# Second feed-forward of a hybrid layer: gate pairs by seven block products, with an up tile ahead of the last two

## What is computed

```python
def swiglu(x, w_gate, w_up, w_down):
    return (jax.nn.silu(x @ w_gate) * (x @ w_up)) @ w_down

x = layer_norm(ALPHA * x + 0.5 * swiglu(x, ffn1_w_gate, ffn1_w_up, ffn1_w_down), ln1_g, ln1_b)
...
x = layer_norm(ALPHA * x + mixed @ w_o, ln2_g, ln2_b)
x = layer_norm(ALPHA * x + 0.5 * swiglu(x, ffn2_w_gate, ffn2_w_up, ffn2_w_down), ln3_g, ln3_b)
```

## Time and profile before

| | |
|---|---|
| median of 3 runs | 2640.41 us |
| the profiled execution | 2638.99 us |
| its span | 2637.2 us |
| TensorE busy, weight loads busy | 98%, 92% of the span |
| VectorE, ScalarE, GpSimd busy | 51%, 31%, 41% |
| mean granted TensorE clock | 0.995 |
| matmuls | 19924 |

### The profile page before, as it was taken

The page is one execution under the profiler, slowest core; times in us unless marked ns, Lnnn a source line. Parts: engine busy times, 40 slices in busy tenths (PEclk is TensorE's granted clock), DMA queues, the critical chain, the costliest instruction groups (busy, mean ns, idle before and its releaser), DMA issues.

```text
span 2637.2 us, 50055 instructions
## 1 busy us (share of the span) xinstructions
PE 2595.3 (98%) x19924; PEld 2432.5 (92%) x19924; DVE 1350.2 (51%) x2181; ACT 807.7 (31%) x1354; POOL 1077.8 (41%) x528
## 2 busy tenths in 40 slices
PE   9999999999999999999999999999999999999997
PEld 9999999998899999999999999999977788888887
DVE  7665554964443452323476655449644435523236
ACT  3222224235532242222252222242355322422222
POOL 4444435413234454434354444354132444544442
PEclk9999999999999999999999999999999999999999
DMA  5333324312233323333233323243122233333332
GB/s 161 95 90 89 88 80 105 81 29 59 60 84 84 104 83 94 88 94 90 80 107 90 96 86 91 80 105 81 27 61 67 76 95 92 96 96 96 96 95 64
DMA packets 457350, 226.58 MB, mean 86 GB/s; under 512 B 42385, under 2 KB 456337, under 8 KB 457201
## 3 DMA queue, kind: packets, MB, share of 16 engines
q1 hardware_dynamic: 450880, 217.09, 29.5%
q10 hardware_dynamic: 6320, 7.41, 1.0%
HBM read 220.20 MB, written 2.10 MB: 84 GB/s over the span
## 4 chain that ended last, share of the span: by engine, by line
PE 88%; DVE 6%; issue 3%; POOL 1%; DMA 1%; ACT 1%; SPq 0%; POOLq 0%; ACTq 0%; DVEq 0%
PE ps L569 74%; PE ps L680 4%; PE ps L592 3%; PE ps L836 1%; PE ps L922 1%; PE ps L961 1%; POOL w_lo L483 1%; DMA w_raw<-in_ffn_w_gate 1%; PE ps L937 1%; PE ps L926 1%; PE ps L843 1%; DVE stat L1727 1%; DVE s_state L1756 1%; DVE s_back L1766 0%; PE ps L939 0%
## 5 line engine op out<-in xcount | busy, mean ns | idle before, releaser
L483 POOL TENSOR_TENSOR w_lo<-w_raw,w_hi 128x1024 fp32r<-128x1024 f32 (+3 forms) x472 | 1038.1, 2205 | 1424.5 <-ACT w_hi L1080 1424.3
L1080 ACT ACTIVATE w_hi<-w_raw 128x1024 fp32r<-128x1024 f32 (+2 forms) x472 | 451.2, 960 | 839.5 <-PE ps L569 642.7
L569 PE MATMUL ps<-x_hi,w_hi 128*128 128x264 f32 (+2 forms) x3584 | 543.6, 302 | 2.0 <-DVE stat L1722 1.7
L569 PE MATMUL ps<-x_hi,w_lo 128*128 128x264 f32 (+2 forms) x3584 | 536.6, 300 | 0.9 <-POOL w_lo L483 0.9
L569 PE MATMUL ps<-x_lo,w_hi 128*128 128x264 f32 (+2 forms) x3584 | 536.3, 300 | 0.0
L569 PEld LDWEIGHTS ps<-x_hi,w_hi 128*128 128x128 f32 x3584 | 481.3, 188 | 29.4 <-issue 3.3
L569 PEld LDWEIGHTS ps<-x_hi,w_lo 128*128 128x128 f32 x3584 | 481.3, 188 | 24.1 <-POOL w_lo L483 1.7
L569 PEld LDWEIGHTS ps<-x_lo,w_hi 128*128 128x128 f32 x3584 | 481.3, 188 | 22.4
L1549 DVE TENSOR_TENSOR hid_rest<-hid_rest,ps 128x528 f32<-128x528 f32 (+1 forms) x88 | 61.6, 699 | 507.2 <-PE ps L569 486.9
L1551 DVE TENSOR_TENSOR hid_lo<-hid_rest,hid_hi 128x528 fp32r<-128x528 f32 (+1 forms) x88 | 224.3, 2548 | 3.1
L1080 ACT ACTIVATE hid_rest<-ps 128x528 f32 (+3 forms) x88 | 53.5, 608 | 354.5 <-PE ps L569 341.1
(11 more groups left out here) (306 smaller groups left out, 2969.5 us busy)
## 6 DMA issues: line engine op xcount, KB each, us to landing
w_raw<-in_ffn_w_gate SPq DMA_DIRECT2D x88, 512.0 KB, 3.8
w_raw<-in_ffn_w_up SPq DMA_DIRECT2D x88, 512.0 KB, 3.8
w_raw<-in_w_in SPq DMA_DIRECT2D x82, 512.0 KB, 3.9
w_raw<-in_ffn_w_down SPq DMA_DIRECT2D x64, 512.0 KB, 4.1
w_raw<-in_ffn_w_down SPq DMA_DIRECT2D x32, 384.0 KB, 3.3
w_raw<-in_w_o SPq DMA_DIRECT2D x16, 512.0 KB, 4.1
w_raw<-in_conv_w_out SPq DMA_DIRECT2D x16, 256.0 KB, 2.8
w_raw<-in_w_in SPq DMA_DIRECT2D x16, 256.0 KB, 2.9
```

The lines of the kernel that those rows point to most:

```text
L483: pool.tensor_tensor(w_lo[:, s, 0:n], w_raw[:, c % RAW, 0:n], w_hi[:, s, 0:n].bitcast(f32), ALU.subtract).then_inc(w_split, 1)
L569: ins = nc.tensor.matmul(dst, w[:, s, cols], x[:, k0 + k, tokens], start=first and k == 0 and n == 0, stop=last and k == n_tiles - 1 and n ...
L1080: return nc.scalar.activation(out, in_, f, **kw)
```

## The change

In the second feed-forward of both layers, two neighbouring gate tiles are made together by Winograd's form of Strassen's scheme: the weights (1024 rows by 256 columns) are cut into two halves of the rows by two tiles, the tokens into two halves, and the 2x2x2 block products become seven. This is done for 10 of the 11 pairs of a layer (`N_CROSS`); the first pair still goes through `first_products`. A block product is 4 weight tiles by 3 passes by 264 (or 256) tokens: 12 matmuls.

VectorE makes four sums of weight blocks for each pair (`add_weights`, L1842, from the raw pair `w_pair` into `w_sum`) and, once for each layer, four sums of input blocks and their low parts (`turn_inputs` and `turned_rest`, L1819 to L1830). It also puts the seven results together in PSUM (`combine`, L1862, five steps). ScalarE saves one result (`crossed_first`), rounds the seven half-size weight chunks and applies silu twice. GpSimd splits seven chunks of 128x512 beside the two up chunks. `w_hi` and `w_lo` become rings of eight half slots (`lay_ring`); ScalarE rounds a chunk when the chunks that held its place are done (`round_at`). For the last group of a part these are: down chunk 0 after block product 5, down chunk 1 after up tile 1, down chunk 2 after block product 7. Loads through `w_raw` keep their rule (two such chunks back must be split), but the gate pairs now have buffers of their own. The L1557 additions are gone; one 128x2112 addition (L1819) does their work ahead of the first product of the feed-forward's VectorE program.

The diff, cut to its core; its pieces are in turn SyncE's loads, TensorE, ScalarE, VectorE before (the removed additions) and VectorE now:

```diff
+FORM_AT, UP_AT = [0, 1, 2, 3, 4, 6, 7], [5, 8]
...
+            def ffn_crossed(l, b0, wg, wu, wd):
...
+                        group += 1
+                        if group < N_CROSS:
+                            load_pair(group)
+                        for j in range(2):
+                            load(l, c + UP_AT[j], 0, 8 * P, rows(wu, l, 0, KD, (f0 + 2 * q + j) * P, P), KD)
...
+            def crossed(l, part, q, a, t0):
...
+                if q == 0:
+                    pe.wait_ge(z_taken, t0 + 1)
+                else:
+                    pe.wait_ge(silu_done, a + 1)
+                pe.wait_ge(turned_ready, l * 4 + 1)
+                form(0, 1, turned(0), True)
+                form(1, 0, own(low, first), True)
...
+                form(2, 3, turned(1), True)
+                pe.wait_ge(turned_ready, l * 4 + 3)
+                form(3, 2, turned(2), True)
+                pe.wait_ge(first_kept, g + 1)
+                form(4, 0, own(high, first), False)
...
+                up(0)
+                pe.wait_ge(turned_ready, l * 4 + 4)
+                pe.wait_ge(crossed_step, 5 * g + 2)
+                form(5, 2, turned(3), False)
+                pe.wait_ge(crossed_step, 5 * g + 3)
+                form(6, 1, own(high, second), False)
+                up(1)
...
                     else:
                         pe.wait_ge(silu_done, n0 + (nf + 2))
+                        if w:
+                            pe.wait_ge(hid_done, n0 + (nf + 1))
                         layer_norm_first(l, 2 * w)
...
+            def ffn_crossed(l, b0):
...
+                        round_at(l, c)
+                        round_at(l, c + 1)
+                        act.wait_ge(chunk_done, done_at(l, c + 1))
+                        ACTV(kept[:, 0:sp.half], ps[:, 0, 0:sp.half]).then_inc(first_kept, 1)
+                        for k in range(2, UP_AT[1]):
+                            round_at(l, c + k)
+                        act.wait_ge(crossed_step, 5 * g + 5)
+                        silu(2 * q, apart(0, sp), 1.0)
+                        silu(2 * q + 1, apart(1, sp), -1.0)
+                        round_at(l, c + UP_AT[1])
...
-                        if w == 1 and part == 0:
-                            for k in ((f,), (f, f + 2))[f >= 4]:
-                                cols = sp.halves[0]
-                                tt(z[:, k, cols], xhf[:, k, cols], xlf[:, k, cols], ADD)
...
+                def turn_inputs():
+
+                    dve.wait_ge(x_ready[0], (n + 2) * KD)
+                    st.done(tt(z[:, :, first], xhf[:, :, first], xlf[:, :, first], ADD))
+                    dve.wait_ge(ln_out[1], (n + 1) * KD)
+                    b11, b12, b21, b22 = z[:, low, first], z[:, low, second], z[:, high, first], z[:, high, second]
+                    follow(tt(raw[:, 0], b11, b12, SUB), turned_made, l * 4 + 1)
...
+                        combine(l * N_CROSS + m, c)
+                        if m < N_CROSS - 1:
+                            add_weights(m + 1, range(4))
+                        hidden(part, f, c + UP_AT[0], 2)
+                        if part == len(PARTS) - 1 and f == nf - 2:
+                            layer_norm_shift(sp)
+                        hidden(part, f + 1, c + UP_AT[1], 3)
```

More of the change, by code:

```diff
@@ L533, in _ @@
                 norm(l, 1, B_FFN2)
-                ffn(l, B_FFN2)
+                for c in range(B_FFN2 + SLOTS, CH):
+                    split(l, c)
                 norm(l, 2, CH)
@@ L679, in last_tiles @@
                             for k in range(nk):
-                                ins = nc.tensor.matmul(ps[:, bank, 0:sp.half], w[:, s, k * P:(k + 1) * P],
+                                ins = nc.tensor.matmul(ps[:, bank, 0:sp.half], held(w, c + d, k * P, (k + 1) * P),
                                                        x[:, k, sp.halves[h]], start=p == 0 and k == 0,
@@ L687, in last_tiles, with form, up @@
                             spread_root(n, 0)
+            def crossed(l, part, q, a, t0):
+                c, g, sp = B_FFN2 + GROUPS_AT[part, q], l * N_CROSS + GROUP_OF.index((part, q)), stream(l)
+                first, second = sp.halves
+                low, high = slice(0, KD // 2), slice(KD // 2, KD)
+                turned = lambda n: [v[:, n, :, 0:sp.half] for v in (turned_hi, turned_lo)]
+                own = lambda k, cols: [v[:, k, cols] for v in (xh, xl)]
+                def form(n, bank, xs, start):
+                    n = FORM_AT[n]
+                    rounded(l, c + n)
+                    for i, (w, x) in enumerate(((w_hi, xs[0]), (w_hi, xs[1]), (w_lo, xs[0]))):
+                        if i == 2:
+                            split_ready(l, c + n)
+                        for k in range(KD // 2):
+                            ins = nc.tensor.matmul(ps[:, bank, 0:sp.half], held(w, c + n, k * P, (k + 1) * P), x[:, k],
+                                                   start=start and i == 0 and k == 0,
+                                                   stop=i == 2 and k == KD // 2 - 1, skip_group_check=True)
+                    ins.then_inc(chunk_done, 1)
+                after_regular = (part, q) == (0, 1)
+                if q == 0:
+                    pe.wait_ge(z_taken, t0 + 1)
+                else:
+                    pe.wait_ge(silu_done, a + 1)
+                pe.wait_ge(turned_ready, l * 4 + 1)
+                form(0, 1, turned(0), True)
+                form(1, 0, own(low, first), True)
+                if q == 0:
+                    pe.wait_ge(z_taken, t0 + 2)
+                elif after_regular:
+                    pe.wait_ge(hid_done, a + 1)
+                else:
+                    pe.wait_ge(silu_done, a + 2)
+                pe.wait_ge(turned_ready, l * 4 + 2)
+                form(2, 3, turned(1), True)
[3 more added lines that the diff above has]
+                form(4, 0, own(high, first), False)
+                def up(j):
+                    if after_regular and j == 0:
+                        pe.wait_ge(silu_done, a + 2)
+                    pe.wait_ge(hid_done, a + (j + 1))
+                    rounded(l, c + UP_AT[j])
+                    product(pair(2 + j, sp), c + UP_AT[j], 0, xh, xl, KD, True, True, split=(l, c + UP_AT[j]),
+                            sp=sp).then_inc(chunk_done, 1)
+                up(0)
[5 more added lines that the diff above has]
+                up(1)
@@ new lines, in gate_up @@
+            def gate_up(l, bu, n0, t0, part, nf):
+                if part:
+                    pe.wait_ge(z_taken, t0 + 1)
+                with loop(pe, 1 if part == 0 else 0, nf // 2) as i:
+                    for j in range(2):
+                        c = bu + 2 * j
+                        rounded(l, c, i * 4)
+                        pe.wait_ge(silu_done, n0 + i * 2 + (j + 1))
+                        product(pair(2 * j), c, 0, xh, xl, KD, True, True, split=(l, c, i * 4)).then_inc(chunk_done, 1)
+                        rounded(l, c + 1, i * 4)
+                        pe.wait_ge(z_taken, t0 + 2)
+                        pe.wait_ge(hid_done, n0 + i * 2 + (j + 1))
+                        product(pair(2 * j + 1), c + 1, 0, xh, xl, KD, True, True, split=(l, c + 1, i * 4)).then_inc(chunk_done, 1)
@@ L699, in ffn @@
                         first_products(l, bu, x0, l * 3 + (1 if w else -1))
[L700 to L711 removed]
+                    if w:
+                        for q in range(1 if part == 0 else 0, nf // 2):
+                            crossed(l, part, q, n0 + 2 * q, t0)
+                    else:
+                        gate_up(l, bu, n0, t0, part, nf)
                     pe.wait_ge(silu_done, n0 + (nf + 1))
@@ L1410, in _ @@
                 layer_norm(l, 1, B_WO)
-                ffn(l, B_FFN2, 1)
+                ffn_crossed(l, B_FFN2)
         @block.vector
```

272 lines of the change are left out of this document (224 added, 48 removed).

## The result

The changed kernel takes 2659.32 us (median of 4 runs, 2658.02 to 2660.97); the kernel before, on the same chip, 2640.35 (2639.57 to 2640.73). The ratio on record is 1.0077, 95% interval 1.0064 to 1.0089 (the two medians alone give 1.0072). So the change makes the kernel slower by 19 us, where 17.2 were forecast. The profiled execution has a span of 2657.5 us.

The account below looks back on a forecast made before the run. The prediction took TensorE, 98% busy, to bound the kernel. Its terms, -26.4 + 14.2 + 20.9 + 2 + 6.5 = +17.2 us on the median 2640.4, gave 2657.6 us; own range 2646 to 2671, with rivals 2627 to 2671.

Parts of the forecast that it names:

- matmuls: Ten gate pairs a layer as seven block products: 1.45 us less each (first layer), 1.19 (last); 26.4 us off.
- starts: Start of each second feed-forward: `x_lo` tiles 4.0 us late, third block product 1.9, later splits and combining 1.1; 14.2 on.
- ends of parts: First down product of each of six parts: TensorE waits 3.1 to 3.85 us for VectorE results behind splits; 20.9 on.
- inside parts: Next group's first block product waits for a late silu: 14 places, 0 to 0.4 us each; 2 us on.
- clock: Half clock for 3.4 us behind five of the six end waits, about 1.3 each; 6.5 us on, bounds 0 and 12.
- outside the second feed-forwards: Rest of the kernel, outside the changed stage: the prediction's sum has no term for it.
- Rival 4: Block matmuls of 256 tokens run slower in the last layer: 2662, or 2689 by the Trainium skill's pace; chance 0.02.
- rival 1: Starts and ends: GpSimd and VectorE miss each other; 3 us a start, 1 an end, no half clock; 2627, chance 0.19.
- Rivals 2 and 3: 2: ends wait, clock holds, `x_lo` tiles not held up, 2643, chance 0.14; 3: VectorE becomes the bound, 2690, chance 0.05.

Follow-up runs that it names:

- e1: Changed kernel, but at the six part ends GpSimd splits down chunk 1 only after VectorE's `hid_lo` of the last tile but one; 2630.39 us.
- e2: Changed kernel, but in the last group of parts 0 and 1 VectorE makes the last tile but one ahead of the four weight sums; 2647.26 us.
- e7: Changed kernel with the edits of e1 and e2 together; 2652.76 us.
- e3: Changed kernel, but TensorE makes all seven block products first and then both up tiles; 2638.64 us.

## Why the prediction was right

| term | predicted | measured |
|---|---|---|
| matmuls | -26.4 | -25.9 |
| starts | +14.2 | +10.7 |
| ends of parts | +20.9 | +21.9 |
| inside parts | +2 | 0 |
| clock | +6.5 | +8.8 |
| outside the second feed-forwards | 0 | about +4 |

The forecast came within 2 us of the measured 19, which is in part luck: the starts (3.5 us) and the inside of the parts (2) cost less than forecast, the clock (2.3), the ends (1.0) and what lies outside the second feed-forwards (4) cost more, and the misses nearly cancel. What was right beyond the number is the mechanism of the largest cost, the ends of parts.

**Matmuls.** The count is the forecast one. From the group spacing in e1, 23.20 - 21.80 = 1.40 in the first layer and 22.24 - 21.05 = 1.19 in the last, ten each. Without its two up tiles (11.12 us) the last layer's group leaves 9.93 us for 84 block matmuls, 0.118 each, the forecast pace. Rival 4, with its 2689 us from the pace of the Trainium skill (TensorE: Matmul & The Clock Gate, section Back-to-back issue gap), is out.

**Ends of parts.** The mechanism is the one forecast, and e1 shows it. The sum is right; the single ends are not: 3.9, 5.9 and 1.5 us in the first layer (forecast 3.3, 3.65, 3.1), 4.8, 3.3 and 2.5 in the last (3.5, 3.85, 3.5). The order of turns that the prediction counted out by instants of 0.2 us came out otherwise: it had one sum behind a split where sums stand at the end, and two were in three of those four ends. So the mean over the six (3.65 measured, 3.48 forecast) held, and no mechanism shown here makes it hold: that is luck too. That they "should fall alike", the reason given against rival 1, was wrong. That the last tile would make no further wait held, but only with the sums ahead of both tiles, where TensorE is late anyway; e2 and e7 put the wait there. Rival 1 (the two engines miss each other) was not what happened, but e1 shows about what it would cost: with no collision ahead of the awaited results at the ends the kernel is at 2630, and rival 1 had 2627, made up otherwise (1 us at each end and 3 at each start; e1 has 1.8 at the ends in all, and its starts still wait).

**Starts.** From the norm's first product to the first down product the stage took 74.45 us before (937.09 to 1011.54) and 81.10 after (939.26 to 1020.36); less the end wait of 3.94 and plus 2 x 1.40 of matmuls this leaves 5.5; in the last layer 5.1. 7.1 each was forecast (its three parts, 4.0, 1.9 and 1.1, add to 7.0). Two parts of the term are mis-sized. The eight `x_lo` tiles took 10.46 us where the forecast's instants give 11.1 (951.36 to 962.5), and TensorE waited 1.22, 0.73 and 0.72 us for the last three, 2.7 and not 4.0. And the third block product, forecast 1.9 late, did not wait; the fourth did, 1.1 us for `turned_lo`. The rest of the 5.5, beyond the 4.1 us of waits that the list has for a layer, is matmuls set further apart at these waits: at 976.17 two runs of four matmuls start 1.84 us apart where 0.48 is usual, 1.36 us more, of which the list counts 1.08.

**Inside a part.** No wait for a silu is in the list: 0, the lower bound.

**Clock.** 23.9 us of TensorE's time in the second feed-forwards are granted at half (1.2 GHz), in four stretches (6.8 us behind three ends, 3.4 behind one). The kernel before has one stretch there, which the earlier trace rows leave out: 3.4 us at the start of the last layer's, behind a wait of 2.11 us; the changed kernel has none at that place.

```profile
2249.00:2250.00 1.00, 1.00 (x7) 0.50 0.10 27
```

By the down projections behind the ends, which take 37.4, 48.6, 38.1, 36.2, 44.6 and 38.3 us where they took 35.0, 46.4, 38.0, 33.7, 44.6 and 36.7, the cost is 8.8. Five stretches of 3.4 us at 1.3 were forecast: one too many, and three of the four were twice as long and cost 2.2 to 2.5 each. The kernel before's stretch falls into the row of the starts. Its matmuls there stand 0.21 us apart instead of 0.12, 17 times, so it cost at most 1.5 us (an estimate); without it the starts would read up to 12.2, and the clock, as a difference of the two kernels, down to 7.3.

**Outside.** The profiled spans differ by 20.3 us. By the starts of the stages 16.2 lie in the second feed-forwards (the table's terms add to 15.5 there), and 4 lie outside of them, where the engines do the same work. The profiles of the changed kernel and its eleven variants, which are alike there too, spend 1869.8 to 1874.5 us outside (each second feed-forward taken from its first matmul to the first of what follows), the changed kernel 1872.8: so much of the 4 us can be scatter between executions. The kernel before, at 1868.6, lies 1.2 us below the lowest of the twelve, so a small cost of the change outside its own stage is not ruled out.

**Rivals 2 and 3.** The clock did fall (rival 2), and VectorE did not become the bound: behind the first group of a layer TensorE never waited for it inside the groups, at 55% busy.

**The range.** The forecast's own range, 2646 to 2671, is said to come with the bounds of start, ends and clock. Those bounds (2 to 18, 0 to 30, 0 to 12, with the matmuls and the 2 us as they are) add up to 2618 to 2676 us; how the narrower range follows from them, the prediction does not show. It held.

## What to carry to other kernels

Before giving VectorE more instructions that read SBUF, look at what GpSimd does in the same microseconds, and count only those instructions that stand between a result and the engine that waits for it: here 22 us of waits and 9 us of clock came from two or three overlaps at each of six places, with the two engines at 55% and 45%. Such a wait can be taken away by one semaphore that lets GpSimd start later (29 us), by ordering the instructions nobody waits for behind both of the results that are needed (25 us), or by giving TensorE more to do in between (e3, 21 us). The first two together do no harm only when the order is changed fully; a half-way order moved the collision to the next result (22 us lost). A start that is one serial chain gained nothing from being held back. Work taken out of that chain, into idle time ahead of it, took 2.5 us off by the medians, which these runs can't tell from nothing.
